# One fp32 transformer kernel: where ScalarE copies the output-gate banks in its gated-memory stage, and in which order it takes eight SiLUs

## The reference, cut to what matters

```
qk = silu(causal_depthwise_conv(concat([mq, mk]), conv_w, conv_b))     # mq, mk: 512 columns each
w[j, s] = exp(a[j] - a[s] + i[s] - m[j])      for s <= j               # a: running sum of log_sigmoid(f)
s[j, s] = (q[j] . k[s]) * 128**-0.5 * w[j, s]
h[j]    = sum_s(s[j, s] * v[s]) / max(|sum_s s[j, s]|, exp(-m[j]))
y_ml    = sigmoid(mo) * head_norm(h)          # mo: another 512 columns of the input projection
```

## Time and profile before

| | |
|---|---|
| median of 3 runs | 1819.75 us (1819.0 to 1820.39) |
| profiled execution, own time | 1820.39 us |
| its span in the trace | 1819.1 us |
| TensorE busy | 1653.1 us (91%) |
| VectorE busy | 727.4 us (40%) |
| ScalarE busy | 478.0 us (26%) |
| GpSimd busy | 317.5 us (17%) |
| mean granted TensorE clock | 0.944 of full speed |
| DMA | 324.30 MB, mean 178 GB/s |

### The profile page before, as it was taken

How to read it: one execution, slowest core, us unless ns; L and a number is a source line. 1 busy time by engine, 2 the same in 40 slices (tenths; PEclk the granted TensorE clock), 3 DMA queues, 4 the chain that set the end, 5 groups by cost and what they waited for, 6 DMA issues and landing times.

```text
span 1819.1 us, 15312 instructions
## 1 busy us (share of the span) xinstructions
PE 1653.1 (91%) x5832; PEld 814.8 (45%) x5832; DVE 727.4 (40%) x1519; ACT 478.0 (26%) x979; POOL 317.5 (17%) x312
## 2 busy tenths in 40 slices
PE   6999999999989699898887787999989999998898
PEld 3544446645454333333333333444455554445553
DVE  2626634254152312111100111459875143996622
ACT  2013242101130010000000001566365134645631
POOL 0000000000000112111101100148143012742500
PEclk9899999999999799898898998989999999899999
DMA  8321032356262599999999998401102130020101
GB/s 322 139 93 46 1 116 93 139 185 236 69 248 87 220 365 408 407 401 409 402 399 403 407 415 325 178 1 70 69 1 88 46 110 0 7 109 24 47 1 46
DMA packets 70960, 324.30 MB, mean 178 GB/s; under 512 B 9290, under 2 KB 12626, under 8 KB 58464
## 3 DMA queue, kind: packets, MB, share of 16 engines
q1 hardware_dynamic: 63552, 308.03, 43.6%
q0 software_dynamic: 6016, 10.51, 1.8%
q10 hardware_dynamic: 1312, 4.72, 0.7%
HBM read 318.95 MB, written 12.67 MB: 182 GB/s over the span
## 4 chain that ended last, share of the span: by engine, by line
PE 68%; DMA 19%; DVE 9%; ACT 2%; issue 2%; POOL 0%; SPq 0%; ACTq 0%; DVEq 0%; POOLq 0%
PE bank L187 65%; DMA arena<-in_w 15%; DMA arena<-h_rows,arena 3%; DVE arena L2454 1%; DVE arena L1214 1%; DVE arena L2438 1%; PE bank L2053 1%; PE bank L567 1%; DVE arena L2495 1%; DVE arena L2508 0%; PE bank L875 0%; DMA arena<-in_params 0%; PE bank L2000 0%; PE bank L662 0%; DVE bank L2486 0%
## 5 line engine op out<-in xcount | busy, mean ns | idle before, releaser
L187 PE MATMUL bank<-arena 128*128 128x512 f32 (+11 forms) x4964 | 1548.0, 551 | 90.6 <-DMA arena<-in_w 53.2
L187 PEld LDWEIGHTS bank<-arena 128*128 128x128 f32 (+3 forms) x4964 | 710.4, 181 | 858.9 <-issue 789.5
L2669 POOL TENSOR_TENSOR arena<-arena 128x512 f32<-128x512 f32 x180 | 205.4, 1141 | 224.1 <-ACT arena L2279 206.6
L1763 POOL TENSOR_TENSOR arena<-arena 128x1 f32<-128x1 f32 (+2 forms) x44 | 32.4, 738 | 682.3 <-DVE arena L1204 456.9
L1711 DVE TENSOR_TENSOR arena<-arena,bank 64x512 f32<-64x512 f32 x32 | 22.1, 691 | 314.2 <-ACT arena L1170 314.2
L2279 ACT ACTIVATE arena<-arena 128x512 f32<-128x512 f32 x180 | 125.9, 717 | 19.6 <-POOL arena L2669 19.3
L959 ACT COPY arena<-bank 128x512 f32<-128x512 f32 (+3 forms) x114 | 60.8, 540 | 228.4 <-PE bank L187 147.3
L1170 ACT ACTIVATE arena<-bank 64x512 f32<-64x512 f32 x32 | 18.9, 591 | 379.6 <-PE bank L187 379.6
L1784 POOL DMA_INDIRECT y_rows<-arena x32 | 32.1, 1004 | 413.4 <-PE bank L875 272.6
L1705 DVE COPY arena<-bank 128x512 f32<-128x512 f32 x32 | 22.1, 692 | 115.2 <-PE bank L875 115.2
L1214 DVE SCALAR_TENSOR_TENSOR arena<-arena 128x512 f32<-128x512 f32 x84 | 63.2, 752 | 3.0
(11 more groups left out here) (264 smaller groups left out, 876.6 us busy)
## 6 DMA issues: line engine op xcount, KB each, us to landing
arena<-in_w SPq DMA_DIRECT2D x96, 2048.0 KB, 34.7
arena<-in_w_in SPq DMA_DIRECT2D x15, 2048.0 KB, 10.8
arena<-in_w_ada SPq DMA_DIRECT2D x12, 2048.0 KB, 8.7
arena<-in_w_out SPq DMA_DIRECT2D x6, 2048.0 KB, 7.7
arena<-in_w_xk SPq DMA_DIRECT2D x2, 2048.0 KB, 9.3
arena<-in_w_xv SPq DMA_DIRECT2D x2, 2048.0 KB, 8.6
arena<-in_w_xq SPq DMA_DIRECT2D x2, 2048.0 KB, 9.9
arena<-in_w_xo SPq DMA_DIRECT2D x2, 2048.0 KB, 9.1
```

The lines of the kernel that those rows point to most:

```text
L187: i = pe.e.matmul(o, l, r, start=first and j == 0, stop=last and j == len(pairs) - 1)
L2669: pool.e.tensor_tensor(yc, yc, k.prod[l][n % 4], ALU.add).then_inc(*k.pool.step("sum", l, f, j))
```

## The change

All of it is on ScalarE. The eight SiLUs are taken in the order of their groups, first the four of the queries and then the four of the keys, instead of query and key of one head in turn. The copy of the "mo" bank of head h stands right behind the exponentials of head h, ahead of the copy of "mlb" of head h+1, instead of behind the copy of "mlb" of head h+1 and ahead of the exponentials of head h+1. For head 3 the place stays the same, behind the squares of the memory rows. `act_mo` is gone; its two lines stand in the loop.

```diff
-    for g in (0, 4, 1, 5, 2, 6, 3, 7):
+    for g in range(8):
         x = (k.MQ if g < 4 else k.MK)[:, g % 4, :]
         act.wait_ge(*V.done("taps", g))
         act.e.activation(x, x, ACT.Silu).then_inc(*A.step("mqk silu", g))
@@
             if phase == 0:
                 act_copy(k, act, NB, B.at("mlb", h), "mlb", h)
-                if h:
-                    act_mo(k, act, h - 1)
             else:
                 act.wait_ge(*V.done("nbm", h))
                 for s in range(4):
@@
                     act.e.activation(k.wt[s][:, lo:lo + 128], NBM[:, lo:lo + 128], ACT.Exp,
                                      bias=bias).then_inc(*A.step("wt", h, s))
-    act_mem_squares(k, act)
-    act_mo(k, act, 3)
-
-
-def act_mo(k, act, t):
-    act_copy(k, act, k.MO[:, t, :], k.banks.at("mo", t), "mo", t)
+                if h == 3:
+                    act_mem_squares(k, act)
+                act.wait_ge(*P.done("mo", h))
+                act.e.copy(k.MO[:, h, :], B.at("mo", h)).then_inc(*A.step("mo", h))
```

## The result

The changed kernel took 1844.03 us (median of 4 timed runs, 1841.62 to 1848.27), the kernel before 1819.67 us (1819.0 to 1820.39): a ratio of 1.0138, 95% interval 1.0121 to 1.0153, or 22 to 28 us slower. All 21 executions of it on record lay between 1840.42 and 1852.1 us. The forecast was 17.6 us slower, 1837.4 us, with 1842 as the upper end of the range. The direction and the place were right, the size was outside.

A forecast was written before the change was run, and what follows sets the result against it. TensorE was taken as the bound (busy 91%, 68% of the wait chain). Waits of 1.57 + 2.64 + 6.92 = 11.1 us plus 6.5 us of low clock gave 17.6 us on 1819.75: 1837.4 us, range 1830 to 1842.

The forecast's parts named there:

- The relay: Heads 0 to 2: "mo" copy, "mlb" copy, mask, products hold TensorE 3.46 us each; cost 2.64 + 6.92 us.
- The SiLU: TensorE's "mls" of head 0 waits for group 4, now fifth: 1.57 us; clock loss 0, upper bound 2.16.
- The clock behind the relays: Low TensorE clock after each of three 3.46 us pauses: 3 x 2.16 = 6.5 us, bounds 0 and 9.9.
- I take the shift as rigid: Behind the stage, everything including the expert weight stream moves later by the same amount: 17.6 us.
- rival 2: Behind the stage, the delay is swallowed in the first waits for weights: about 1820 us, no change; chance 0.04.
- rival 3: Only head 0's part shows, VectorE's products getting ahead for heads 1 and 2: 4.2 us, 1824 us; chance 0.04.
- rival 4: Low-clock stretches at 304 to 622 and 1107 to 1816 us fall elsewhere, making it faster: 1810 us; chance 0.02.

The follow-up runs named there:

- Products first: The changed kernel with VectorE's four score products of head h moved ahead of the mask of head h+1: 1823.39 us, ratio 1.0012.
- work in the pauses: The changed kernel with four extra 128x512 matmuls on TensorE behind "mo" of each of heads 0 to 2: 1837.57 us, ratio 1.01.
- second profile of before: The kernel before, with no edit, profiled once more: 1821.36 us (12 runs).
- The two pure delays: The kernel before with 23 or 20 extra 128x512 matmuls on TensorE ahead of the value products of head 3: 1842.93 and 1835.63 us.
- second profile of the changed kernel: The changed kernel, with no edit, profiled once more: 1843.4 us (5 runs), ratio 1.0113.
- the changed kernel with 1.25 matmuls more: The changed kernel with one 128x512 and one 128x128 matmul added ahead of the value products of head 3: 1841.45 us, ratio 1.0109.

## Why the prediction was wrong

**The relay: right.** The order of the chain, its place and its length were as worked out: 3.46 forecast, 3.48, 3.57 and 3.57 measured, the extra 0.1 being TensorE's own start after VectorE. Only three of them, none for head 3. "Products first" shows the link by the mask as the cause.

**The SiLU: the wait right, its clock wrong.** This is a term of the sum that I put at nothing. Five SiLUs stand in the chain and the first score product moved as forecast (263.05 less the late start of 5.8 is 257.25, against 257.3). But I wrote for that pause "I take 0 for it and keep one loss of 2.16 as upper bound", by the nearest pause of 0.82 us, which left the clock at 1.00. It was 1.44 us long (I had said about 1.8) and cost 1.7 in both profiles of the changed kernel, 2.9 in that of "work in the pauses". The upper bound was near the truth. That a pause even shorter is no safeguard shows ahead of the stage, in TensorE's timeline of the changed kernel:

```profile
208.27 1.12 PE L187 MATMUL bank<-arena 64*128 64x512 f32 x2 [0.90 <-ACT arena L1000]
...
239.49 1.12 PE L187 MATMUL bank<-arena 64*128 64x512 f32 x2 [0.90 <-ACT arena L1000]
```

In the first profile of before the same two pauses of 0.90 us had full clock behind them (1.00 from 160 to 254.5 us); here both belong to the stretch that averages 0.95.

**The clock behind the relays: right.** 6.5 us forecast with a mean loss of 2.16; the three took 1.7, 1.5 and 2.8, together 6.0. Work put into the pauses removed it (clock 1.00 from 263.5 to 319.6 us), so the pause is its cause. The rule of the Trainium skill ("TensorE: Matmul & The Clock Gate", the section on oscillation), by which every turn of a waiting loop pays anew, holds in this case for all three.

**"I take the shift as rigid": wrong.** This is the step that failed. The waits behind the stage were rigid: the piece of 55.44 us is the same and so is the pause of 2.40 us. The delay reached the end, so rival 2 is out, and three relays came, so rival 3 is out. The clock was not. TensorE's own later pauses, unchanged in length, meet the low clock or escape it according to when they come, and a delay moves them. With the delay of the changed kernel the long form came in both profiles, 4.4 us more than in the second profile of before. I had this as rival 4, but priced it as a gain only and gave it 2 in 100; the same mechanism as a loss was in no case and not in the range. The two pure delays show it without any other change, in profiles that met the clock alike ahead of the stage. In the timed runs it is less sure: the first interval, 22 to 28 us, leaves out the stage's 19.4, the second, 17 to 24 us, takes it in.

The first profile of before hid it, as it had the long form behind the stage already, paid for by the short form ahead of it. So the match between the two spans' 25.2 us and the first median's 24.4 is in part luck: the extra 5.8 us stood ahead of the stage, where no cost of the change can stand. For an execution like the second profile of before, the sum as it should have stood is 17.6 + 1.7 + 4.4 = 23.7, near the 22.5 to 24.4 of the medians. The same page of the Trainium skill says, in Part 1, that the number of slow matmuls at the start differs from run to run of one kernel; read as a warning about every pause, it would have told me that one profile can't give the clock term of a delayed kernel. What stays open is the rest: from the first expert rows on, the second profile of the changed kernel took 4.1 us more than that of before (1847.4 - 655.0 against 1820.1 - 631.8), the first one did not (1844.3 - 655.5 = 1188.8), and with so few profiles I can't say that this is more than scatter.

## What to carry to other kernels

In an engine with an in-order stream, a copy that waits for long work must not stand ahead of one whose data are ready, if a third engine has something behind the second: look for what is queued behind each wait, two engines on. A pause on a dense TensorE stage costs its length and, if the clock falls, half of the low-clock stretch behind it: here 1.7 or 2.9 us behind a pause of 1.44, and 1.5 to 2.8 behind one of 3.5. And take two profiles of the kernel before: if they differ in where the clock is low, add an uncertainty of that size on both sides of any shift.

## What the runs showed of the hardware

The same program had full clock from 160 to 254.5 us in one profile and 0.95 in another, 5.5 us apart at the same instruction, with the same pauses of 0.90 to 1.25 us. Its timed runs spread from 1812.56 to 1827.48 us on one chip. In profiles that met the clock alike ahead of the stage, a delay of 17.1 us of dense matmuls left the piece of 139.3 us behind it as it was, one of 19.7 us made it 143.3, and one of about 20.4 us (the changed kernel with 1.25 matmuls more) left it at 139.3 too; behind the same pause of 2.40 us the same 160 records took 62.44 or 65.83 us. An edit of 1 to 3 us can thus move a later piece of this kernel by 4 us.
